# Inverse softmax sums: sent through DRAM in one attention stage, turned once per pair in the other

## The reference

```
s = einsum('bqkgd,bnkd->bkgqn', q, k) * scale
p = softmax(s, axis=-1)
o = einsum('bkgqn,bnkd->bqkgd', p, v)
y = (o.reshape(...) * silu(g)) @ w_out        # layer 0; layer 1 is alike with its windows
x = x + gate * y                              # after layer 1: rms_norm(x, final_g)
```

## Time and profile before

| what | value |
| --- | --- |
| median of 3 runs | 1556.99 us (1556.64 to 1563.7) |
| profiled execution | 1555.47 us |
| its span, first to last instruction | 1553.7 us |
| mean granted TensorE clock | 0.987 of full speed |
| PE, DVE, ACT, POOL busy | 1504.4, 1001.2, 813.9, 434.1 us |
| bytes moved | 252.24 MB, of which 8.39 MB from ACT's queue |

### The profile page before, as it was taken

The page is one execution under the profiler, slowest core; times in us unless marked ns, Lnnn a source line. Parts: engine busy times, 40 slices in busy tenths (PEclk is TensorE's granted clock), DMA queues, the critical chain, the costliest instruction groups (busy, mean ns, idle before and its releaser), DMA issues. The chain is left out here.

```text
span 1553.7 us, 26405 instructions
## 1 busy us (share of the span) xinstructions
PE 1504.4 (97%) x9547; PEld 1320.2 (85%) x9547; DVE 1001.2 (64%) x2144; ACT 813.9 (52%) x1869; POOL 434.1 (28%) x507
## 2 busy tenths in 40 slices
PE   6999999999999999989999999999997999999998
PEld 3787878897998899978888888889997889999996
DVE  4665636428888888863448966575222887777783
ACT  5322321127777777755554433343112987777773
POOL 1022201002222111100121333220480554555552
PEclk9899999999999999999999999999998999999999
DMA  9444425409111254023233444579857998999872
GB/s 361 141 136 141 144 82 177 159 18 272 25 25 24 86 157 136 17 91 102 81 123 120 134 140 144 151 211 289 263 137 238 289 290 256 264 254 267 255 227 68
DMA packets 195654, 252.24 MB, mean 162 GB/s; under 512 B 32979, under 2 KB 157477, under 8 KB 195493
## 3 DMA queue, kind: packets, MB, share of 16 engines
q1 hardware_dynamic: 193076, 242.16, 51.4%
q10 hardware_dynamic: 2448, 8.39, 1.8%
HBM read 187.59 MB, written 78.76 MB: 171 GB/s over the span
## 5 line engine op out<-in xcount | busy, mean ns | idle before, releaser
L2537 DVE CUSTOM_DVE_ANT_0 nprob<-nS,bias_set 128x640 f32<-128x640 f32 x128 | 105.2, 822 | 68.3 <-PE nS L2375 45.6
L1152 ACT ACTIVATE prob<-S,nm,qk_inv 128x512 f32<-128x512 f32 (+1 forms) x208 | 146.4, 707 | 3.5 <-DVE nm L1088 3.5
L576 PE MATMUL pp<-h_hi,w_hi 128*128 128x512 f32 (+1 forms) x408 | 147.5, 361 | 0.0
L577 PE MATMUL pp<-h_lo,w_hi 128*128 128x512 f32 (+1 forms) x408 | 144.5, 354 | 0.0
L578 PE MATMUL pp<-h_hi,w_lo 128*128 128x512 f32 (+1 forms) x408 | 144.4, 354 | 0.0
L1106 DVE TENSOR_TENSOR ptlo<-TB,pthi 128x512 fp32r<-128x512 f32 (+1 forms) x192 | 114.8, 598 | 29.7 <-ACT pthi L1164 27.9
L2456 ACT CAST npt_hi<-nTB 128x256 fp32r<-128x256 f32 (+1 forms) x256 | 103.3, 426 | 56.8 <-PE nTB L2386 53.1
L1164 ACT CAST pthi<-TB 128x512 fp32r<-128x512 f32 (+1 forms) x192 | 99.2, 517 | 63.1 <-PE TB L1033 62.9
L1081 DVE TENSOR_REDUCE mx<-S 128x1 f32<-128x512 f32 (+1 forms) x208 | 116.7, 580 | 10.6 <-PE S L1025 9.4
L2550 DVE TENSOR_TENSOR npt_lo<-nTB,npt_hi 128x256 fp32r<-128x256 f32 (+1 forms) x256 | 114.9, 483 | 2.6 <-ACT npt_hi L2456 1.4
L2447 ACT ACTIVATE nprob<-nprob,selector 128x640 f32<-128x640 f32 x128 | 106.6, 833 | 11.4 <-DVE selector L2537 10.4
(11 more groups left out here) (324 smaller groups left out, 4519.9 us busy)
## 6 DMA issues: line engine op xcount, KB each, us to landing
kq_scratch<-p_stage SPq DMA_DIRECT2D x96, 256.0 KB, 3.9
keys<-kq_scratch SPq DMA_DIRECT2D x32, 768.0 KB, 4.8
bias_set<-bias_scratch SPq DMA_DIRECT2D x64, 384.0 KB, 6.3
v_strip<-v_scratch SPq DMA_DIRECT2D x128, 128.0 KB, 5.3
wearly<-in_mod_w SPq DMA_DIRECT2D x15, 1024.0 KB, 8.2
bias_scratch<-bias_wide_scratch SPq DMA_DIRECT2D x16, 768.0 KB, 11.0
w_raw<-in_na_w_in SPq DMA_DIRECT2D x11, 1024.0 KB, 5.5
wside<-in_mod_w SPq DMA_DIRECT2D x9, 1024.0 KB, 7.1
```

The source lines that it names most:

```text
L576: pe.matmul(acc, whi[:, k, ws], hi[:, k, a:a + width], start=(k == 0), stop=False)
L577: pe.matmul(acc, whi[:, k, ws], lo[:, k, a:a + width], start=False, stop=False)
L1152: act.activation(prob[:, p % 5, a:a + n], S[:, score_bank(p, k), 0:n], ACT.Exp, bias=nm[:, p % 5:p % 5 + 1], scale=q_scale(h - 1, p) if p ...
```

## The change

In the grouped attention the two turns and DVE's copy of each group go. ACT stores the group's two columns of inverse sums (128 partitions of 8 bytes) to a DRAM row at the end of its iteration p = 2 gr + 4, and at the end of the next iteration, once the store has landed, loads that row of 256 numbers back onto all 128 partitions. `inv_sums` has two buffers, and DVE's multiplication reads it with a stride of two, as the row has the tiles interleaved. In the last stage POOL copies the inverse sums of a unit's two heads into one tile (64 columns of each), and PE turns that tile, once per unit instead of once per group. ACT's copy of them, POOL's gate multiplication and POOL's last multiplication are done once per unit on 128 partitions, too. ACT's fold of a unit's first head waits for POOL's last multiplication of the unit before. The gate rows get semaphores and two buffers of their own, and SP asks for them after the unit's second bias load.

```diff
-        inv = c.sb("inv_sums", [P, 256])
+        inv = c.sb("inv_sums", [P, 2, 256])
...
+        def inverse_row(n):
+
+            return io["inv_row"][n % GQA_GROUPS]
+
+        def inverses_moved(eng, sems, n):
+
+            eng.wait_ge(sems[n % 2], 16 * (n // 2 + 1))
...
-                        at_least(pe, recd, GQA_GROUPS, h, gr)
                         at_least(pe, od, GQA_GROUPS, h, gr - 1)
-                        for s in range(2):
-                            pe.transpose(O[:, 256 + s * P:256 + (s + 1) * P],
-                                         rec[:, q - 1 + s:q + s].broadcast_to([P, P]), consts["ident"][:, :])
...
+                    if GQA_GROUPS * h + gr >= GQA_GROUPS:
+                        inverses_moved(dve, inv_out, GQA_GROUPS * (h - 1) + gr)
                     dve.reciprocal(rec[:, q:q + 2], tot[:, q:q + 2]).then_inc(recd, 1)
...
-                    dve.tensor_copy(inv[:, :], O[:, 256:512]).then_inc(invd, 1)
-                    at_least(dve, invd, GQA_GROUPS, h, gr)
-                    dve.tensor_tensor(qk[:, bass.ds(head, 1), tok:tok + 256].rearrange("p a n -> p (a n)"),
-                                      O[:, 0:256], inv[:, :], ALU.mult).then_inc(od, 1)
+                    n = GQA_GROUPS * h + gr
+                    inverses_moved(dve, inv_in, n)
+                    dve.tensor_tensor(qk[:, bass.ds(head, 1), tok:tok + 256].rearrange("p a (s n) -> p (a s) n", s=2),
+                                      O[:, 0:256].rearrange("p (s n) -> p s n", s=2),
+                                      inv[:, n % 2, :].rearrange("p (n s) -> p s n", s=2), ALU.mult).then_inc(od, 1)
...
+                def store_inverses(h, gr):
+
+                    n, q = GQA_GROUPS * h + gr, (2 * gr) % GQA_N
+                    at_least(act, recd, GQA_GROUPS, h, gr)
+                    if n >= GQA_GROUPS:
+                        inverses_moved(act, inv_in, n - GQA_GROUPS)
+                    act.dma_start(inverse_row(n).rearrange("(p s) -> p s", s=2), rec[:, q:q + 2]).then_inc(inv_out[n % 2], 16)
+
+                def load_inverses(h, gr):
+
+                    n = GQA_GROUPS * h + gr
+                    inverses_moved(act, inv_out, n)
+                    if n >= 2:
+                        act.wait_ge(od, n - 1)
+                    act.dma_start(inv[:, n % 2, :], inverse_row(n).rearrange("(a n) -> a n", a=1).broadcast_to([P, 256])
+                                  ).then_inc(inv_in[n % 2], 16)
...
+                        if live((p - 4) // 2, prev, tail):
+                            if p % 2 == 0:
+                                store_inverses(h, (p - 4) // 2)
+                            else:
+                                load_inverses(h, (p - 5) // 2)
...
+                def gate_in(u):
+                    s, i, slot = u // PAIRS, u % PAIRS, u % 2
+                    if u >= 2:
+                        sp.wait_ge(gid, u - 1)
+                    sp.dma_start(g[:, slot, :], io["gl"][i, :, s * 256:s * 256 + 256]).then_inc(gin[slot], 16)
...
-                    vg_in(u)
+                    v_in(u)
                     if u + 1 < UNITS:
                         bias_in(2 * u + 3)
+                    gate_in(u)
...
+                def spread_inverses(u):
+
+                    pe.wait_ge(repd, 2 * u + 2)
+                    if u:
+                        pe.wait_ge(invd, u)
+                    for f in range(HALVES):
+                        pe.transpose(O[:, 1, 256 + f * P:256 + (f + 1) * P],
+                                            both[u % 2][:, f, :, :].rearrange("p a n -> p (a n)"), consts["ident"][:, :])
...
-                        pe.wait_ge(recd, 2 * gr + 2)
                         if gr >= 2:
                             pe.wait_ge(sumd, gr - 1)
-                            pe.wait_ge(invd, gr - 1)
-                        for r in range(2):
-                            at = (2 * gr + r) % 8
-                            pe.transpose(O[:, gr % 2, 256 + r * P:256 + (r + 1) * P],
-                                         rec[:, at:at + 1].broadcast_to([P, P]), consts["ident"][:, :])
+                        if a == 1:
+                            spread_inverses(gr // 2)
...
-                        act.wait_ge(od, gr - 1)
-                    act.copy(inv[rows(a), :], O[rows(a), gr % 2, 256:512]).then_inc(invd, 1)
+                        act.wait_ge(od, gr // 2)
+                    if a == 1:
+                        act.copy(inv[:, :], O[:, 1, 256:512]).then_inc(invd, 1)
                     act.copy(half[rows(a), :], O[rows(1 - a), gr % 2, 0:256]).then_inc(halfd, 1)
...
+                def replicate(gr):
+                    if gr >= 2 * UNITS:
+                        return
+                    u, a = gr // 2, gr % 2
+                    pool.wait_ge(recd, 2 * gr + 2)
+                    if u >= 2:
+                        pool.wait_ge(pvd, 2 * u - 2)
+                    at = 2 * gr % 8
+                    pool.tensor_copy(both[u % 2][:, :, a, :],
+                                     rec[:, at:at + 2].unsqueeze(2).broadcast_to([P, HALVES, 64])).then_inc(repd, 1)
+                    pool.wait_ge(repd, gr + 1)
+
+                replicate(0)
+                replicate(1)
+                for u in range(UNITS):
+                    s, i, slot = u // PAIRS, u % PAIRS, u % 2
+                    if u:
+                        pool.wait_ge(old, u)
+                    swap(u + 2)
+                    if u >= 12 and u % 4 == 0:
+                        root(u // 4 - 3)
+                    replicate(2 * u + 2)
+                    pool.wait_ge(invd, u + 1)
+                    pool.wait_ge(gin[slot], 16 * (u // 2 + 1))
+                    pool.tensor_tensor(inv[:, :], inv[:, :], g[:, u % 2, :], ALU.mult).then_inc(gid, 1)
+                    pool.wait_ge(gid, u + 1)
+                    replicate(2 * u + 3)
+                    pool.wait_ge(sumd, 2 * u + 2)
+                    pool.tensor_tensor(o[:, :], half[:, :], inv[:, :], ALU.mult).then_inc(od, 1)
```

More of the change, by code:

```diff
@@ L950, in grouped_attention @@
         topd = c.sem("g_max_raw")
-        totd, recd, gated, invd = c.sem("g_total"), c.sem("g_recip"), c.sem("g_gated"), c.sem("g_inv")
+        totd, recd, gated = c.sem("g_total"), c.sem("g_recip"), c.sem("g_gated")
+        inv_out, inv_in = ([c.sem(f"g_inv_{x}{i}") for i in range(2)] for x in ("stored", "loaded"))
         td, hid, lod = c.sem("g_turned"), c.sem("g_pt_hi"), c.sem("g_pt_lo")
@@ L1165, in high @@
                              TB[:, no % 2, 0:n].rearrange("p (b q) -> p b q", q=P)).then_inc(hid, 1)
+                def store_inverses(h, gr):
[11 more added lines that the diff above has]
+                                  ).then_inc(inv_in[n % 2], 16)
                 def body(h, kv, kvp, tail=False):
                     prev = kvp is not None
-                    for p in range(LAG if tail else GQA_N):
+                    for p in range(LAG + 1 if tail else GQA_N):
                         q = p - LAG
@@ L2249, in neighbourhood_and_out @@
             inv, o = (c.sb(f"n_{x}", [P, 256]) for x in ("inv", "o"))
+        with c.place((205.5, 207)):
+            both = [both0, c.sb("n_rec_both1", [P, HALVES, 2, 64])]
         vs = c.sb("v_strip", [P, 2, 6, 256], F32R)
@@ L2269, in neighbourhood_and_out @@
         meand, rootd, late, switched = c.sem("x2_mean"), c.sem("x2_root_done"), c.sem("x2_late_root"), c.sem("root_table_in")
-        lated = c.sem("x2_late_recip")
+        gin = [c.sem(f"gate_in{i}") for i in range(2)]
+        lated, repd = c.sem("x2_late_recip"), c.sem("n_rec_spread")
         x_last, st_last = [c.sem(f"x1_last_in{b}") for b in range(2)], [c.sem(f"x_last_stored{b}") for b in range(2)]
@@ L2394, in product @@
                     if not second:
-                        pe.wait_ge(recd, 2 * gr + 2)
                         if gr >= 2:
                             pe.wait_ge(sumd, gr - 1)
-                            pe.wait_ge(invd, gr - 1)
-                        for r in range(2):
-                            at = (2 * gr + r) % 8
-                            pe.transpose(O[:, gr % 2, 256 + r * P:256 + (r + 1) * P],
-                                         rec[:, at:at + 1].broadcast_to([P, P]), consts["ident"][:, :])
+                        if a == 1:
+                            spread_inverses(gr // 2)
                         pe.wait_ge(lod, 4 * gr + 4)
                         if gr % 2 == 0:
-                            pe.wait_ge(vl[slot], 96 * (gr // 4 + 1))
+                            pe.wait_ge(vl[slot], 80 * (gr // 4 + 1))
                     work_ = [[(4, 4, 0, 256), (5, 5, 0, 256), (1, 1, 0, 256)],
@@ L2542, in reciprocal @@
                     dve.wait_ge(expd, p + 1)
+                    if p >= 8:
+                        dve.wait_ge(repd, p // 2 - 3)
                     dve.reciprocal(rec[:, p % 8:p % 8 + 1], sums[:, p % 8:p % 8 + 1]).then_inc(recd, 1)
@@ L2648, in _ @@
                 swap(1)
```

(18 more changed lines are left out.)

8 lines of the change are left out of this document (3 added, 5 removed).

## The result

The changed kernel took 1576.87 us in the median (1574.98 to 1578.01) against 1556.99: a ratio of 1.0125 with a 95% interval of 1.0105 to 1.0146. It is slower by 19.9 us where 11 us less was forecast, and it lies outside the range of 1539 to 1557 us. In what follows a trip is the way of one group's inverse sums, ACT's store and the load behind it; a landing is the time from a transfer's issue to its completion; a burst is a row of transfers that SP issues without a pause. The profiled execution has a span of 1573.2 us, 19.5 us more than before.

A forecast was written before the change was run, and what follows sets the result against it. TensorE, busy 97% of the span, was taken as the bound. Attention -5.0 and last stage -6.0 gave -11.0 us, from 1555.5 to 1544.5 profiled, stated as 1546 for the runs' median; range 1539 to 1557.

The forecast's parts named there:

- the round trip's term for SP's bursts: Grouped attention: SP's bursts of transfers meet some eight or nine groups' stores and loads, costing +0.5 us, bounds 0 and 7.
- rival (c): Grouped attention: the store lands too late and ACT stalls; 1563 us for 4.5 us landings, 1579 for 5; chance 0.10.
- The issue terms: Grouped attention: each DMA issue stops ACT 0.5 us; within +5.0 us at iteration 3's end, and +0.8 at one thinly covered place.
- The pair and DVE's chain: Grouped attention: 40 pairs of PE turns saved, -8.8 us; PE's idle behind DVE's copy gone once per head, -3.5 us.
- The strided multiplication: Grouped attention: DVE's multiplication reading inverse sums with a stride of two words was taken to keep its time of today.
- The end of the stage: Grouped attention, last group: two landings of about 2.6 us with no next head to hide in, +1 us.
- The last stage: Last stage: 32 fewer pairs of PE turns, -5.3 us in strips 2 to 4 and -0.7 in the first, -6.0 in sum.
- (a): Whole kernel: everything is covered, the issue at iteration 3 and the end cost nothing; -16 us, 1541; chance 0.22.
- (b): The attention gives nothing, through a second ACT-bound point per head; only the last stage gains; 1551 us; chance 0.18.
- (d): Last stage: POOL is late with a copy and PE waits up to 1 us per unit, 32 us at most; chance 0.04.

The follow-up runs named there:

- kernel 5: The changed kernel with SP's table fills and small bias transfers paced and its 16 transfers of 768 KB moved into the third stage: 1547.97 us, ratio 0.9942.
- Kernel 7: The kernel before, turns and copies kept, plus ACT's 40 stores and 40 loads with their waits into a buffer nobody reads: 1592.33 us, ratio 1.0223.
- Kernels 1: Only the attention half of the change, with the last stage of the kernel before: 1583.46 us, ratio 1.0165.
- 8: The changed kernel with the load and its wait for the store on POOL's queue instead of ACT's, bursts as they were: 1583.78 us, ratio 1.0165.
- kernel 2: Only the last stage's half of the change, with the grouped attention of the kernel before: 1550.78 us, ratio 0.9954.

## Why the prediction was wrong

**The step that failed** is the round trip's term for SP's bursts: "+0.5 us, bounds 0 and 7 (the nine groups at the 4.6 us of rival (c))". It measured about +27 us: the first seven heads of the kernel after sum to 306.1 us, those of kernel 5, with the bursts away, to 279.4, and 25.6 of the 26.7 lie in the three heads with bursts. A near row was there, the 8.6 us for 512 KB in the crowded last stage against 4.0 us for 640 KB in the quiet, but I scaled that delay by the size of my own transfer ("a quarter the size or less takes maybe a microsecond more"). The delay belongs to the crowd, not to the transfer: 1 KB took 9.3 us. A nearer row stood inside the two bursts themselves, the landings of their own 768 KB transfers (L876) in the kernel before:

```profile
DMA to landing us min/median/max: 6.2/11.0/12.4
```

The upper bound rests on landings of 4.6 us, an estimate from the Trainium skill's 2 us for HBM under load (DMA: Bandwidth & Descriptors, Latency and other measured facts); the six stores measured 7.7 to 11.6, so the measurement decides against that estimate. The 3.0 to 6.1 us by which the packets start late are no part of it. Nor does the bound of 7 follow: by rival (c)'s own working nine groups at 4.6 us cost about 4.5 us. No term, moreover, was put down for TensorE's clock, though PE stood for 3 to 4 us at a stretch in each of those three heads, and up to 11 of the 27 us are what the clock took with that. And the range closed at 1557 because the mechanism of rival (c), right in kind (ACT waiting for its own store with the stage behind it), was priced above that only as one landing time for all 40 groups. Six stores that landed in 7.7 to 11.6 us are enough.

**The issue terms are zero:** 3.5 of the +5.0 (seven times 0.5) and the +0.8. The other 1.5 of the +5.0 is the pair's gain given back at iteration 3, which came true (next paragraph). An issue took 0.33 us, inside the bounds, but it does not stop ACT, contrary to the prediction: it runs beside ACT's work. Kernel 7 shows heads of 41.22 and 41.25 us with ten issues each.

**The pair and DVE's chain, -8.8 and -3.5.** In a head the two give 1.0 us, not 1.54, or 1.32 after what is given back. The starts of the exponentials in kernel 5 against those before show where: 0.22 us after the third, 0.22 after the fifteenth, 0.22 from the twentieth to the twenty-second, 0.35 before the last. At the end of iteration 3, where PE waits for ACT's high part, the pair gives nothing, as the prediction had it (from turn to turn 5.89 us in kernel 5, 5.88 before). The strided multiplication takes 416 ns against 424 (L1122 against L1115), so the choice of its old time was right. The sum of these terms over the first seven heads is -6.2 us measured; the prediction's, with the issues in it (a head of -1.10 - 0.44 + 0.72 + 0.10 = -0.72 us), was -5.0. That this came out close is luck: a term too large stood against one that did not exist.

**The end of the stage, +1**, was +2.8 to +3.0, and +4.3 against the same kernel without the last two trips. I had only followed the last group; the last but one also holds ACT, before the cast that the last product needs.

**The last stage, -6.0**, was right: -6.7 alone. In the kernel after its strips give 3.5 us, where alone they give 5.0, and in kernel 5 the stage is 6.5 us shorter than before; one execution each does not tell whether these differ.

**The rivals.** (a) and (b) fail with the bursts in place. Without the bursts and without the last two trips the change gives 15.4 us. That it is near (a)'s 16 is luck: in that kernel's profile the first seven heads give 5.5 us, not 10.8, and the end of the attention gives 1.5. (c) was the right mechanism at the wrong extent. (d) did not happen. The change did what it says.

The sum with the measured terms: -6.2 for the heads, +26.7 for the bursts, +3.0 for the end, -3.5 for the last stage is +20.0 us, where the spans differ by 19.5.

## What to carry to other kernels

Before a dependence goes through DRAM, list what every other queue does in the same microseconds, and take a small transfer's landing from the crowd's rows, unscaled: here its size bought nothing (in the bursts 1 KB landed in 7.7 to 11.6 us, the crowd's own 768 KB in 6.2 to 12.4 before). Price the worst landings and not the median, because engines that wait in order pass a late one on, and add what the clock takes when PE has stood for some microseconds. If the crowd has no deadline, move it to where no trip runs: here that turned a loss of 19.9 us into a gain of 8.8, and leaving the last two trips out made it 15.4.

## What the runs showed of the hardware that was not expected

- A store of 1 KB in 128 runs of 8 bytes lands in 2.5 to 3.7 us in the quiet (kernel after, heads 6 and 7 up to the end), little more than the 2.2 to 3.5 us of 15 KB in 64-byte runs, and in 7.7 to 11.6 us beside a burst on the other queue.
- The trips slow the burst in turn: SP's eight transfers took 18.98 and 20.11 us to issue, before 14.05 and 15.47, with only 1 KB and 128 KB transfers added. Kernels 1, 7 and 8, with trips, show 19.14 to 21.34 us; kernel 2, without them, 14.62 and 15.05.
- An issue on ACT's queue (0.33 us) lies under a running exponential and costs ACT nothing.
- Three times in the kernel after, beside a pause of PE of 3.3 to 4.1 us, the granted clock fell to 0.50 for 3.41 to 10.24 us, most of it with matmuls running again.
